# Stage borders made by halves of the tokens, and own steps for each cross attention head

## What is computed

```
for l in 0, 1:  x = LN1(a*x + 0.5*swiglu(x)); x = LN2(a*x + mixer(x)); x = LN3(a*x + 0.5*swiglu(x))
for l in 0, 1:
    h = h + rms(mix_l(rms(h) * g_mix_pre)) * g_mix_post
    h = h + rms(cross(rms(h) * g_x_pre, mem)) * g_x_post
    h = h + rms(relu(rms(h) * g_ff_pre @ w1)**2 @ w2) * g_ff_post
```

## Time and profile before

| | us |
|---|---|
| median of 3 runs (lowest, highest) | 3543.58 (3542.51, 3544.23) |
| the profiled execution | 3545.09 |
| its span, first to last instruction | 3543.3 |
| PE busy | 3382.5 (95%) |
| PE weight loads busy | 2787.9 (79%) |
| DVE busy | 1780.8 (50%) |
| ACT busy | 1329.8 (38%) |
| POOL busy | 62.1 (2%) |
| mean granted clock of PE | 0.975 of full speed |

### The profile page before, as it was taken

The page is one execution under the profiler, slowest core; times in us unless marked ns, Lnnn a source line. Parts: engine busy times, 40 slices in busy tenths (PEclk is TensorE's granted clock), DMA queues, the critical chain, the costliest instruction groups (busy, mean ns, idle before and its releaser), DMA issues.

```text
span 3543.3 us, 38158 instructions
## 1 busy us (share of the span) xinstructions
PE 3382.5 (95%) x15620; PEld 2787.9 (79%) x15620; DVE 1780.8 (50%) x2721; ACT 1329.8 (38%) x2106; POOL 62.1 (2%) x64
## 2 busy tenths in 40 slices
PE   8999989999999999899999899999999889999998
PEld 6888767888878887778888678767888778768886
DVE  4333684533453336844334775546444665645444
ACT  3222554322242225543322554334332565434231
POOL 0000000000000000000000000000000000000000
PEclk9999999999999999999999999999999999999999
DMA  4333311333323332113333233212333313213332
GB/s 147 101 96 89 78 48 54 101 95 98 94 84 100 96 89 72 50 52 105 109 95 95 61 106 96 83 50 76 101 100 95 84 54 95 72 42 107 99 98 66
DMA packets 604286, 304.10 MB, mean 86 GB/s; under 512 B 43600, under 2 KB 601808, under 8 KB 603984
## 3 DMA queue, kind: packets, MB, share of 16 engines
q1 hardware_dynamic: 604112, 301.66, 29.7%
HBM read 299.52 MB, written 2.10 MB: 85 GB/s over the span
## 4 chain that ended last, share of the span: by engine, by line
PE 78%; DVE 13%; ACT 7%; DMA 1%; issue 1%; SPq 0%; DVEq 0%; ACTq 0%
PE ps L1599 24%; PE ps L1600 24%; PE ps L1607 24%; DVE wl L1986 2%; DVE Y L2159 1%; PE ps L1623 1%; PE ps L1616 1%; ACT wh L1771 1%; DVE tmp L1995 1%; DVE XR L2082 1%; ACT XH L1813 1%; PE ps L1756 1%; PE ps L1657 1%; DVE XL L2068 1%; ACT tmp L1840 1%
## 5 line engine op out<-in xcount | busy, mean ns | idle before, releaser
L1599 PE MATMUL ps<-XH,wh 128*128 128x512 f32 x2600 | 1047.5, 403 | 52.3 <-ACT XH L1813 14.6
L1607 PE MATMUL ps<-XL,wh 128*128 128x512 f32 (+1 forms) x2856 | 1065.2, 384 | 0.0
L1600 PE MATMUL ps<-XH,wl 128*128 128x512 f32 x2600 | 1025.4, 394 | 0.0
L1986 DVE TENSOR_TENSOR wl<-raw,wh 128x1024 fp32r<-128x1024 f32 (+1 forms) x565 | 680.2, 1209 | 531.4 <-ACT wh L1771 531.2
L1771 ACT ACTIVATE wh<-raw 128x1024 fp32r<-128x1024 f32 (+1 forms) x565 | 584.0, 1039 | 560.1 <-PE ps L1607 495.0
L1607 PEld LDWEIGHTS ps<-XL,wh 128*128 128x128 f32 x2856 | 544.4, 191 | 106.0
L1599 PEld LDWEIGHTS ps<-XH,wh 128*128 128x128 f32 x2600 | 496.8, 191 | 163.3 <-issue 35.9
L1600 PEld LDWEIGHTS ps<-XH,wl 128*128 128x128 f32 x2600 | 497.4, 191 | 103.5 <-issue 2.2
L1599 PE MATMUL ps<-HHa,wh 128*128 128x512 f32 x1088 | 427.6, 393 | 9.2 <-DVE HLa L1990 5.8
L1600 PE MATMUL ps<-HHa,wl 128*128 128x512 f32 x1088 | 423.6, 389 | 0.0
L1607 PE MATMUL ps<-HLa,wh 128*128 128x512 f32 x1088 | 408.0, 389 | 0.0
(11 more groups left out here) (322 smaller groups left out, 3060.3 us busy)
## 6 DMA issues: line engine op xcount, KB each, us to landing
raw<-in_ffn_w_gu SPq DMA_DIRECT2D x176, 512.0 KB, 3.8
raw<-in_w_ff SPq DMA_DIRECT2D x128, 512.0 KB, 4.1
raw<-in_ffn_w_down SPq DMA_DIRECT2D x64, 512.0 KB, 4.0
raw<-in_w_xkv SPq DMA_DIRECT2D x32, 512.0 KB, 3.9
raw<-in_ev_w_in SPq DMA_DIRECT2D x25, 512.0 KB, 3.8
raw<-in_ffn_w_down SPq DMA_DIRECT2D x32, 384.0 KB, 3.4
raw<-in_w_in SPq DMA_DIRECT2D x24, 512.0 KB, 3.9
raw<-in_w_out SPq DMA_DIRECT2D x64, 128.0 KB, 2.7
```

Of the source, the lines that this page charges most:

```text
L1599: e.matmul(bank[:, 0:n], t.wh[u % SPL][:, k, :], h, start=first, stop=False)
L1600: e.matmul(bank[:, 0:n], t.wl[u % SPL][:, k, :], h, start=False, stop=False)
L1607: m = e.matmul(bank[:, 0:n], t.wh[u % SPL][:, k, :], l, start=False, stop=last)
L1986: self.e.tensor_tensor(wl, raw, f32(wh), ALU.subtract).then_inc(self.s["lo"], self.tag("lo", f"lo.{i}"))
```

## The change

The last four of a stage's eight columns are made in two passes (`tail`): first for tokens 0 to 255 of all four, then for tokens 256 to 511, with matmuls of 256 tokens, two columns in one PSUM bank. The sums of the first half and its spread are put into the second pass, and so are the first two half tiles of the norm. At the start of the next stage the three columns are made by half as well (`project_halves`, `finish_border`): for each half eight steps of nine matmuls. The norm's instructions are on half tiles. The four weight buffers are held by the tail's units until their second pass; `split_next` splits the next stage's units one at a time at set places. The squares for `pre_scale` are now made in it. In the cross attention each head has its own generator, all are advanced together, up to three times at each tile. Six borders are layer norms, six post norms; the last has no next stage.

```diff
@@ class Border @@
+    def take(self, p, h, bank, key, first):
+        w, m = self.w, 4 + 2 * p
+        if self.stats is None:
+            self.stats = w.stats if self.ln else w.ystats
+            self.stats.fold("dve")
+            self.k1, self.k2 = [self.stats.k1] * 2, [self.stats.k2] * 2
+        k = f"{self.k}.take{p}{h}"
+        self.got[p, h] = k
+        if self.ln:
+            w.p_residual2(k, m, h, bank, first, (key, w.xr[m], w.xr[m + 1]))
+        else:
+            w.p_to_y2(k, m, h, bank, first, (key, w.y_free if first else (w.ys[m], w.ys[m + 1])))
+        w.psum.give(bank, k)
+        src = (w.t.XR if self.ln else w.t.Y)[:, m:m + 2, HALF[h]]
+        q, f = w.tmp.take()
+        a = w.square(q[:, :].rearrange("p (a t) -> p a t", a=2), src, k, f)
+        self.q[p, h] = (q, a)
+        if self.ln:
+            for i in range(2):
+                s1 = self.stats.s1[:, HALF[h]]
+                self.k1[h] = w.sum_pool(s1, s1, w.t.XR[:, m + i, HALF[h]], (self.k1[h], k))
...
+    def sums(self, h):
+        w, st = self.w, self.stats
+        tb, bf = w.psum.take()
+        if self.ln:
+            t1 = w.column_sums(tb, 1, 2, 0, 2, st.s1[:, HALF[h]], (self.k1[h], bf))
+        t2 = w.column_sums(tb, 1, 0, 0, 2, st.s2[:, HALF[h]], (self.k2[h], bf))
+        if h:
+            if self.ln:
+                w.tmp.give(st.s1, t1)
+            w.tmp.give(st.s2, t2)
...
+    def tile(self, m, h):
+        w, (bank, t) = self.w, self.bank[h]
+        k = f"{self.k}.{m}.{h}"
+        kind, name, l, nxt = self.spec
+        if self.ln:
+            q, f = w.tmp.take()
+            g, b = w.t.vec(f"{name}_g", l * KD + m), w.t.vec(f"{name}_b", l * KD + m)
+            old = w.xr[m] if m < 4 else self.got[m // 2 - 2, h]
+            w.p_bn_scale(k, m, h, q, bank, (t, f, old))
+            w.p_bn_affine(k, m, h, q, g, b, nxt is None, self.x_free[m])
+            w.tmp.give(q, f"{k}.x")
+        else:
+            old = w.ys[m] if m < 4 else self.got[m // 2 - 2, h]
+            w.p_post_scale(f"{k}.y", m, h, bank, w.t.vec(name, l * KD + m), (t, old))
+        self.flush()
+        if not self.ln:
+            w.p_post_add(f"{k}.x", m, h, (f"{k}.y", w.xr[m]))
+        if nxt:
+            g = w.t.vec(nxt[0], nxt[1] * KD + m)
+            w.p_scaled_hi(k, m, h, g, (f"{k}.x", self.x_free[m]))
+            self.pend = lambda: w.p_scaled_lo(k, m, h, g, self.x_free[m])
+        elif self.ln:
+            self.pend = lambda: w.p_bn_lo(k, m, h, self.x_free[m])
+        if m == KD - 1:
+            w.psum.give(bank, f"{k}.q" if self.ln else f"{k}.y")
+    def flush(self):
+        if self.pend:
+            self.pend()
+        self.pend = None
@@ class Walk @@
+    def split_next(self):
+        if self.units_in is None or self.n_split >= len(self.units_in):
+            return
+        while self.n_loaded < min(len(self.units_in), self.n_split + RAW):
+            self.load_unit(self.n_loaded)
+            self.n_loaded += 1
+        self.split_unit(self.n_split)
+        self.n_split += 1
...
-            if f[2] >= f[1]:
-                f[2] -= f[1]
-                next(f[0], None)
+            for _ in range(f[3]):
+                if f[2] >= f[1]:
+                    f[2] -= f[1]
+                    next(f[0], None)
...
+    def half_steps(self, us, src, h, name):
+        for k, x in enumerate(src):
+            self.p_first(us, k, H, k == 0, x[0], x[-1])
+            self.p_last(us, k, H, k == len(src) - 1, x[1], x[2], name)
+            yield
+    def tail(self, w, src, k0, get, take, first, spec):
+        for m in range(4):
+            bank, t = get(m)
+            self.psum.give(bank, take(m, bank, t, first, True))
+        base, nk = self.u, len(src)
+        units = [self.next_unit(w, m * P, k0, nk, base) for m in range(4, KD)]
+        b = Border(self, take, spec)
+        halves = [[(x[0][:, s], x[1][:, s], x[2], x[-1]) for x in src] for s in HALF]
+        for p in range(2):
+            bank, f = self.psum.take()
+            for i in range(2):
+                for _ in self.half_steps([(units[2 * p + i], bank[:, HALF[i]], f)], halves[0], 0, ".a"):
+                    pass
+            b.take(p, 0, bank, f"mm.{units[2 * p + 1]}.a", first)
+            if p == 0:
+                b.fold(0, 0)
+        b.fold(1, 0)
+        n = 0
+        for p in range(2):
+            bank, f = self.psum.take()
+            for i in range(2):
+                for _ in self.half_steps([(units[2 * p + i], bank[:, HALF[i]], f)], halves[1], 1, ""):
+                    n += 1
+                    if n == 9:
+                        b.sums(0)
+                        self.split_next()
+                    if n == 18:
+                        b.spread(0)
+                        b.tile(0, 0)
+                        b.tile(1, 0)
+            b.take(p, 1, bank, f"mm.{units[2 * p + 1]}", first)
+            if p == 0:
+                b.fold(0, 1)
+                self.split_next()
+        self.split_next()
+        b.leave()
+        if spec[3] or self.ln_next(spec):
+            self.border = b
+        else:
+            self.border = None
+            self.finish_border(b, [])
...
+    def finish_border(self, b, us):
+        steps = [iter(())] * 2
+        if us:
+            steps = [self.half_steps([(u, bank[:, HALF[h]], free) for u, bank, free in us], b.halves(h), h,
+                                     "" if h else ".a") for h in range(2)]
+        old, self.xr = self.xr, b.old_xr
+        b.tile(2, 0)
+        b.fold(1, 1)
+        b.tile(3, 0)
+        b.tile(4, 0)
+        for _ in range(4):
+            next(steps[0], None)
+        b.sums(1)
+        if us:
+            self.split_next()
+        for m in (5, 6, 7):
+            b.tile(m, 0)
+        for _ in range(3):
+            next(steps[0], None)
+        b.spread(1)
+        for m in range(KD):
+            b.tile(m, 1)
+        b.flush()
+        for g in steps:
+            for _ in g:
+                pass
+        self.xr = old
+    def project_halves(self, cols, b):
+        base = self.u - 1
+        us = []
+        for w, c0 in cols:
+            u = self.next_unit(w, c0, 0, KD, base)
+            us.append((u, *self.psum.take()))
+        self.finish_border(b, us)
+        return [(bank, f"mm.{u}") for u, bank, free in us]
...
     def pre_scale(self, nxt):
 
-        self.stats.fold_held()
+        st = Stats(self, False)
+        for m in range(KD):
+            st.add(self.t.XR[:, m, :], self.xr[m])
+            if m == 4:
+                self.split_next()
+        st.fold("dve")
         nxt.ahead()
-        steps = self.stats.finish_steps(D, RMS_EPS)
+        steps = st.finish_steps(D, RMS_EPS)
         next(steps)
         nxt.ahead()
         next(steps)
...
@@ cross @@
+        def head(h):
+            while len(tq) < 2 * h + 2:
+                yield
+            yield
+            for b in range(NB):
+                yield
+                score(h, b)
+                yield
+            yield
+            for b in range(NB):
+                norm(h, b)
+            yield
+            for b in range(NB):
+                yield
+                turn(h, b)
+            for j in range(2):
+                yield
+                yield
+                value(h, j)
         def steps():
-            for n in range(4 * NB + 7):
-                while n < 4 * NB and len(tq) < 2 * (n // NB) + 2:
-                    yield
-                if 0 <= n - 5 < 4 * NB:
-                    norm(*divmod(n - 5, NB))
-                if n < 4 * NB:
-                    score(*divmod(n, NB))
-                if 0 <= n - 6 < 4 * NB:
-                    turn(*divmod(n - 6, NB))
-                if n >= 10 and (n - 10) % NB == 0:
-                    yield
-                    value((n - 10) // NB)
+            live = [head(h) for h in range(4)]
+            while live:
+                for g in list(live):
+                    try:
+                        next(g)
+                    except StopIteration:
+                        live.remove(g)
...
-                self.fill_with(steps(), EVERY3, DELAY3)
+                self.fill_with(steps(), 1, 0, LEAD)
```

More of the change, by code:

```diff
@@ L19 @@
 NB = 4
+H = T // 2
+HALF = (slice(0, H), slice(H, T))
 ALPHA = float(4.0 ** 0.25)
@@ L791, in to_hidden, with out_project @@
         return outs
-    def out_project(self, w, take, order=None, finish=None):
-        nxt = self.stream([(w, m * P) for m in range(KD)], self.hs)
+    def out_project(self, w, take, norm, order=None, finish=None):
+        nxt = self.stream([(w, m * P) for m in range(4)], self.hs)
         nxt.start(order)
@@ L798, in out_project @@
             finish()
-        for m in range(KD):
-            bank, t = nxt()
-            self.psum.give(bank, take(m, bank, t, True, True))
+        t = self.tail(w, self.hs, 0, lambda m: nxt(), take, True, norm)
         for s in range(KD):
@@ L2084, in p_gated, with p_to_y2 @@
+    def p_to_y2(self, k, m, h, bank, first, after):
```

(7 more changed lines are left out.)

254 lines of the change are left out of this document (124 added, 130 removed).

## The result

The changed kernel takes 3630.2 us in the median (3629.0 to 3631.1), the kernel before 3543.1 beside it: ratio 1.0247, 95% interval 1.0235 to 1.0259, 87 us slower. Predicted were 3616, within 3555 to 3650. The profiled execution has a span of 3627.5 us, 84.2 more than before, at a mean clock of 0.974.

The account below looks back on a forecast made before the run. Borders were to be bound by VectorE, level with TensorE before and slower on half tiles. From 3545.1 profiled, +28 layer norm, +25 post norm, +7 prescale, +22 clock, -10 cross attention gave 3617, median 3616; range 3555 to 3650.

Parts of the forecast that it names:

- (1) and (2): Halved last columns: half a takes 11.5 us in four columns; half b ends at 24.8 with sums and broadcast.
- (3) and (4): Next stage's start: TensorE waits 3.4 us for the third unit's split weights, then 4.2 for tile 4's low half.
- Rival A: Borders: the waits do not come and the 8.4 us earlier start holds, kernel faster at 3505; chance 0.14.
- (5): Second half's eight half tiles in a border come at VectorE's pace, 1.17 us each (post norm 1.38).
- The borders at full clock: Fifth column to third next column: 54.7 us after a mixer, 51.8 after an FFN, 53.0 post norm; +28 and +25.
- The clock: Half steps slowed at TensorE's 1.2 GHz level, two or three per border, +2 at eleven borders: +22 us, bounds 0 and 66.
- Rival B: TensorE's clock stays at the upper level through waits of 3 to 4 us: 3594; chance 0.18.
- Rival C: Lower clock holds through most of the next stage's half steps, 66 for 22: 3660; chance 0.10.
- Prescale: Squares and sums now follow the border, ending 6.6 us after it against one column of 5.4: +1.2, six times, +7.
- Cross attention: Each head going on by itself saves 5 us in each of two layers, -10; bounds -13 and +10.
- rival D: The cross attention steps bring nothing or cost 10 us: 3626 to 3636; chance 0.10.
- The last border: Border without a next stage: nothing gained, normed tiles end 38.2 us after the fifth column's start, for 38.5 before.

Follow-up runs that it names:

- Run 8: Kernel before, only the matmuls of each stage's last four columns made as two of 256 tokens: 3558.1 us (1.0043).
- run 4: Changed kernel with third split before the last take, tile 4's low half before the second sums, fourth split later, fewer constant matmuls in waits: 3597.3 us (1.0151).
- run 5: Kernel of Run 3 without the layer norm's subtraction of the mean (output differs, timing only): 3583.0 us (1.0112).
- Run 3: Changed kernel with constant matmuls, never read, put on TensorE where it waits in a border: 3602.0 us (1.0163).
- run 9: Kernel before with only the change's own steps for each cross attention head: 3536.0 us (0.9973).
- run 11: Kernel before with the change's cross steps and constant matmuls inside the column sums, ahead of the broadcast and behind it: 3521.8 us (0.9941).
- run 10: Kernel before with the change's cross steps and constant matmuls, 8 (post norm 4) before the broadcast, 12 (11) behind it: 3526.5 us (0.9954).
- Run 7: Changed kernel with the prescale's eight squares put back into the border, their seven sums still behind it: 3625.3 us (1.0231).

## Why the prediction was right, and where it was not

The sign and, within 14 us of 87, the size came out. The stretches that it named are all longer than it said: 58.3 and 58.4 after a mixer for 55 to 57, 54.4 to 55.9 after an FFN for 52 to 54, 54.9 to 57.3 in a post norm for 53 to 55 (windows less 0.16). By its steps:

**The halved tail, steps (1) and (2).** Half b ends 24.9 after the start (24.8 foreseen) behind a mixer, 19.0 (19.1) behind an FFN. Run 8 gives the price of the matmuls alone, 14.5.

**The waits of (3) and (4).** They are there, 3.12 and 3.89 us (3.4 and 4.2 foreseen), and 3.17 and 2.75 in a post norm (3.3 and 3.0). After an FFN the third unit starts 26.0 us after the border (386.44 - 360.46) where its weights were foreseen at 25.8. But the step that says that the earlier start is given back *to these waits* and to the pace is wrong in its first half. With constants in the idle places, moving the causes of both brought 4.7 us in eleven borders (run 4), against 72 if they had cost their length. They are where TensorE feels VectorE's chain, and they go elsewhere when moved. Rival A did not happen, as the waits came. What it took for granted, that an earlier split and an earlier low half would keep the early start, is not borne out either: run 4 has both and stands at 3597, not near 3505. That no order of this kind could get there is not shown.

**The pace of (5)** is the part that holds: 1.18 measured for 1.17, 1.40 for 1.38 in the post norm (2338.51 - 2337.11), and run 5 shows it as a cause: 18 us out of six borders for 0.34 us less per half tile, nothing in the other five. The Trainium skill's rule that the prediction weighed (VectorE: DVE Perf Modes, "The TRN2 errata") is borne out by this case: half as many elements cost 0.42 us of duration for 0.69.

**The borders at full clock** were summed to 54.7, 51.8 and 53.0. Run 3 has 55.5, 52.5 to 53.1 and 53.5 (windows less 0.16). Over eleven, 589.1 for 581.6: 7.5 too little.

**The clock** was put at +22; run 3 prices it at 28. Its size was near, its working was not: the term set slow half steps against VectorE's pace, while run 3 finds the cost in VectorE's two waits, for the sums and for the broadcast that stand behind slow steps. Rival B (the clock stays, 3594) is refuted by the windows at 0.50; with the clock held the kernel takes 3602, 8 more than B said, which is what the borders at full clock were summed too short. Rival C (3660) did not come either: the windows have 0.88 to 0.94 in the mean. But as a difference between the kernels the term is too large. The kernel before pays too: from run 9 to the best filling is 14 us, and not all of its borders are held there. With the same cross steps, the two kernels are 3630.2 - 3536.0 = 94 apart as they are, and 3602.0 - 3521.8 = 80 with filled waits: about 14 go to the clock, and less if the five borders not held in run 11 were held too. The rest stands in the border terms, which I had set against borders of before that were slow themselves: behind a mixer, 55.5 has to be set against 21.8 + 27.1 = 48.9, +6.6 and not +2.9 (+7.5 against run 10's 26.24). So the split of the loss between borders and clock, as the prediction had it, is not right, although its total is.

**Prescale.** The column sums start 2347.74 - 2341.10 = 6.64 us behind the border, where the column alone takes 24 x 0.227 = 5.4: the 1.2 foreseen. Run 7 brought 5 us net, with longer borders against it; by the spans, 84.2 - 87.1 + 8.2, what stands outside the borders and the cross attention cost 5.3, for the 7 foreseen.

**Cross attention.** -10 foreseen; -4.1 per layer in the windows, -7.5 by itself (run 9), so rival D is out. The stretch that the prediction named can't be compared: the first output column now starts 36.7 us into it, with head steps still to come, which is why the windows run to the fifth. **The last border:** nothing, as foreseen. VectorE's last operation ends 38.1 us after the start of the fifth column, for 38.5 before.

The miss is then 7.5 (borders) + 6 (clock) + 2.5 (cross) - 2 (prescale) = 14, with the terms as the prediction cut them. It is no proof of each: the clock term's 28 is a gain of constants that were put in, and they may cost something themselves.

## What to carry to other kernels

Before work is cut in halves to overlap it, count the operations of the engine that feeds the border: VectorE was already level with TensorE there, and each half-sized operation costs it 0.34 to 0.45 us, where one of twice the size costs 0.60 to 0.68. A wait in the list of TensorE may be only where another engine's chain shows; move its cause with the clock held before you price it, and look in the windows whether the clock was held. And a filled wait is a cheap trial: constant matmuls in existing idle places won 28 us here and 14 in the kernel before.

## What the runs showed of the hardware

The granted clock can fall while TensorE has no gap: in run 10's first border it is busy 29.49 of 29.49 us, and falls within 32 one-column matmuls. The Trainium skill (TensorE: Matmul & The Clock Gate, "HAM oscillation") speaks of bursts with waits between them; here there was no wait. What made it fall is open: the next border has the same 32 rows and keeps 1.00, and four constants among them did not keep it in run 11's first border. And half speed on TensorE cost the border after the mixer nothing where VectorE did its own tiles (3.16 us at 0.50 and at 1.00), but 2.9 us where the sums and the broadcast stood behind slow steps.
